# Two transformer blocks on one core: the order of long and short products within a weight slot of an FFN

## What is computed

```
u, g = split(h @ w_up)            # 1024 x 2816 each
g = causal_dwconv(g)              # 3 taps
y = (silu(g) * u) @ w_down        # 2816 x 1024
```

```
y = (silu(x @ wg) * (x @ wu)) @ wd
```

## Time and profile before

| | us |
|---|---|
| median of 3 runs | 1596.24 |
| lowest, highest | 1596.08, 1598.06 |
| the profiled execution, its own time | 1598.12 |
| its span, first to last instruction | 1596.4 |
| busy: TensorE | 1578.2 (99%) |
| busy: VectorE | 1090.8 (68%) |
| busy: ScalarE | 920.0 (58%) |
| busy: GpSimd | 56.7 (4%) |

### The profile page before, as it was taken

The page is one execution under the profiler, slowest core; times in us unless marked ns, Lnnn a source line. Parts: engine busy times, 40 slices in busy tenths (PEclk is TensorE's granted clock), DMA queues, the critical chain, the costliest instruction groups (busy, mean ns, idle before and its releaser), DMA issues.

```text
span 1596.4 us, 23557 instructions
## 1 busy us (share of the span) xinstructions
PE 1578.2 (99%) x9239; PEld 1355.2 (85%) x9239; DVE 1090.8 (68%) x1759; ACT 920.0 (58%) x1553; POOL 56.7 (4%) x98
## 2 busy tenths in 40 slices
PE   7999999999999999999999999999999999999998
PEld 6888888889888888888887788888888889888887
DVE  5877776778676767665677466567666667775665
ACT  5756755567665546644476564457454484674544
POOL 4010000000030000000002100000000000000000
PEclk9999999999999999999999999999999999999999
DMA  8555666555356555666655465665666664456662
GB/s 286 161 158 171 221 226 193 186 163 166 114 182 200 192 186 182 200 187 189 192 164 168 122 204 180 199 191 164 215 190 187 186 198 147 120 177 202 188 188 77
DMA packets 212401, 288.20 MB, mean 181 GB/s; under 512 B 11096, under 2 KB 180382, under 8 KB 212292
## 3 DMA queue, kind: packets, MB, share of 16 engines
q1 hardware_dynamic: 208500, 280.00, 55.6%
q0 software_dynamic: 3792, 6.70, 1.6%
HBM read 284.99 MB, written 3.88 MB: 181 GB/s over the span
## 4 chain that ended last, share of the span: by engine, by line
PE 94%; DVE 2%; DMA 1%; ACT 1%; issue 0%; SPq 0%; POOL 0%; DVEq 0%
PE two L2211 88%; PE two L2288 1%; PE two L2457 1%; DVE w_lo L1483 1%; PE two L2470 1%; DMA x_tok<-in_x 1%; PE two L2480 1%; DVE qk L1839 1%; PE two L2840 0%; PE two L2274 0%; DMA vals<-u_dram 0%; ACT w_hi L864 0%; PE two L2483 0%; DMA u_dram<-aux 0%; DVE misc L1817 0%
## 5 line engine op out<-in xcount | busy, mean ns | idle before, releaser
L2211 PE MATMUL two<-act_parts,w_hi 128*128 128x512 f32 (+1 forms) x2784 | 803.4, 353 | 0.0
L1483 DVE TENSOR_TENSOR w_lo<-raw,w_hi 128x1024 fp32r<-128x1024 f32 (+1 forms) x520 | 612.9, 1220 | 114.7 <-ACT w_hi L864 114.2
L2211 PE MATMUL two<-act_parts,w_lo 128*128 128x256 f32 x2256 | 637.2, 282 | 0.0
L2211 PEld LDWEIGHTS two<-act_parts,w_hi 128*128 128x128 f32 x2784 | 487.6, 189 | 80.8 <-issue 5.4
L864 ACT CAST w_hi<-raw 128x1024 fp32r<-128x1024 f32 (+1 forms) x520 | 516.3, 1048 | 7.0 <-DMA raw<-in_ffn_w_up 4.7
L2211 PEld LDWEIGHTS two<-act_parts,w_lo 128*128 128x128 f32 x2256 | 425.4, 189 | 2.1
L2211 PE MATMUL two<-w_hi,act_parts 128*128 128x512 f32 (+2 forms) x832 | 247.1, 377 | 3.1 <-ACT w_hi L864 3.0
L993 ACT COPY p_sb<-two 128x512 f32<-128x512 f32 x108 | 62.7, 580 | 243.0 <-PE two L2211 243.0
L2211 PE MATMUL two<-w_hi,hid_even 128*128 128x512 f32 x576 | 185.7, 390 | 0.0
L2211 PEld LDWEIGHTS two<-w_hi,act_parts 128*128 128x128 f32 x832 | 151.0, 189 | 32.6 <-ACT w_hi L864 3.4
L1611 DVE TENSOR_TENSOR pt_sb<-two,p_sb 128x512 f32<-128x512 f32 x54 | 37.3, 691 | 194.5 <-ACT p_sb L993 194.5
(11 more groups left out here) (317 smaller groups left out, 1191.9 us busy)
## 6 DMA issues: line engine op xcount, KB each, us to landing
raw<-in_ffn_w_up SPq DMA_DIRECT2D x160, 512.0 KB, 4.1
raw<-in_ffn_w_down SPq DMA_DIRECT2D x132, 512.0 KB, 3.5
raw<-in_ffn_w_gate SPq DMA_DIRECT2D x80, 512.0 KB, 3.8
raw<-in_a_w_in SPq DMA_DIRECT2D x24, 512.0 KB, 4.9
raw<-in_fox_w_in SPq DMA_DIRECT2D x20, 512.0 KB, 3.8
raw<-in_ffn_w_up SPq DMA_DIRECT2D x32, 256.0 KB, 3.7
raw<-in_w_kv SPq DMA_DIRECT2D x12, 512.0 KB, 4.2
raw<-in_mem_w_kv SPq DMA_DIRECT2D x8, 512.0 KB, 11.3
```

Of the source, the lines that this page charges most:

```text
L1483: nc.vector.tensor_tensor(slot(w_lo, t, n), slot(raw, t, n), slot(w_hi, t, n), ALU.subtract).then_inc(lo_done, 1)
L2211: return nc.tensor.matmul(dst, a, w, start=start, stop=stop, skip_group_check=True)
```

## The change

It reorders the products of a slot in `gate_or_up` for s of 2 and more: first the eight long products of the slot, in the order (k, m), and then its eight short products in the same order. For s = 1 the order stays as it was. The number, the operands and the outputs of the products stay the same, each has its LDWEIGHTS as before, and the increment stays on the slot's last product, a short one in both kernels.

```diff
@@ -2336,18 +2336,20 @@
                         t = gate_slots(f, s) + 2 * part + i
                         slot_ready(t)
                         hi, lo = whole_slot(t, 4)
-                        for k in range(4):
-                            for m in range(2):
-                                c, w = 4 * i + k, slice(m * P, (m + 1) * P)
-                                if s == 1:
-                                    d = gate_up(part)[:, m * SEQ:(m + 1) * SEQ]
-                                    mm(d, hi[:, k, w], act_parts[:, 0, c, :], c == 0 and m == 0, False)
-                                    mm(d, hi[:, k, w], act_parts[:, 1, c, :], False, False)
-                                else:
-                                    d = gate_up_wide(part)[:, m * HALF:m * HALF + SEQ]
-                                    mm(gate_up_wide(part)[:, m * HALF:(m + 1) * HALF].rearrange("p (a t) -> p a t", a=2), hi[:, k, w],
-                                       act_parts[:, :, c, :], c == 0, False)
+                        tiles = [(k, 4 * i + k, m, slice(m * P, (m + 1) * P)) for k in range(4) for m in range(2)]
+                        if s == 1:
+                            for k, c, m, w in tiles:
+                                d = gate_up(part)[:, m * SEQ:(m + 1) * SEQ]
+                                mm(d, hi[:, k, w], act_parts[:, 0, c, :], c == 0 and m == 0, False)
+                                mm(d, hi[:, k, w], act_parts[:, 1, c, :], False, False)
                                 ins = mm(d, lo[:, k, w], act_parts[:, 0, c, :], False, c == NCH - 1)
+                        else:
+                            for k, c, m, w in tiles:
+                                mm(gate_up_wide(part)[:, m * HALF:(m + 1) * HALF].rearrange("p (a t) -> p a t", a=2), hi[:, k, w],
+                                   act_parts[:, :, c, :], c == 0, False)
+                            for k, c, m, w in tiles:
+                                ins = mm(gate_up_wide(part)[:, m * HALF:m * HALF + SEQ], lo[:, k, w], act_parts[:, 0, c, :], False,
+                                         c == NCH - 1)
                         ins.then_inc(gu_full if i else w_tm, 1)
 
                 def down(s, b, halves=(0, 1)):
```

## The result

The changed kernel takes 1599.29 us (median of 20 runs), the kernel before 1597.06 beside it: a ratio of 1.0015, 95% interval 1.0008 to 1.0021. It is slower by about 2.2 us, where 1591.3, a gain of 4.9 us, was forecast.

A forecast was written before the change was run, and what follows sets the result against it. TensorE was taken as the bound, busy 1578.2 of 1596.4 us. Rows of like products gave -9.9 and entries +5.0, together -4.9 us, median 1591.3; own range 1587.5 to 1593.5, with rivals 1585 to 1601.5.

The forecast's parts named there:

- Step (1): In a slot's row of eight long products: 0.2267 us each, 1.814 a row, from down steps; bounds 0.22 and 0.24.
- The price of 0.006: In gate and up's alternating order: each long-short pair pays some 0.006 us for the change of length, over 1728 pairs.
- the pair of 0.34: In the alternating order: one pair took 0.34 us, matching 0.2267 and 0.1187, so two segments carry no fixed price.
- Step (2): In a slot's row of eight short products: 0.1187 us each, 0.950 a row, with weight loads hidden.
- Step (3): At 168 entries from shorts into rows of longs: 0.03 us each, +5.0 us; the way back costs nothing.
- Step (4): At slot releases and their readers on SyncE, ScalarE and VectorE: starts 0.02 us earlier a slot, cost nothing.
- Rival B: In a slot's longs: they keep 0.2325 us in a row, entries add 0.03 each; slower, 1601.2 us, chance 0.22.
- Rival A: In gate and up slots: order doesn't matter, a slot stays at 2.81 us, median 1596.2; chance 0.2.
- The rule that the prediction took from the Trainium skill: For TensorE's product distances: columns over 2.4 GHz and 2.5 ns, so a pair is 0.325 in any order, change worth nothing.

The follow-up runs named there:

- alike_new: Changed kernel with the gate and up weight slots placed like all others, a move of 32 columns: 1593.46 us, ratio 0.9977 against the kernel before.
- act_moved: Changed kernel with weight slots unmoved and the activations moved by 32 columns: 1595.51 us beside 1596.81 for the kernel before, a single run.
- adjacent_new: Changed kernel with a chunk's hi and lo activations side by side in SBUF: 1599.2 us, ratio 1.0013 against the kernel before.
- adjacent_old: Kernel before, longs and shorts in turn, with a chunk's hi and lo activations side by side in SBUF: 1596.85 us, ratio 1.0000.
- sweep_new: Changed kernel with a different pair of places for the high and low weights of gate and up in each FFN: 1594.75 us, a single run.
- mixed_new: Changed kernel with only `w_hi` of steps 2 to 10 placed like all other slots: 1595.4 us, ratio 0.9991 against the kernel before.
- quarter_new: Changed kernel with gate and up slots at a third place, 16 columns from either other: 1587.11 us, ratio 0.9941 against the kernel before.
- snake: mixed_new with shorts first in the second slot of each part: 1590.33 us, ratio 0.9959 against the kernel before.
- quarter_snake: quarter_new with shorts first in the second slot of each part: 1583.89 us, ratio 0.9919 against the kernel before.

## Why the prediction was wrong

**Step (1), eight long products in a row, failed.** It took 0.2267 from the down steps, "the row with most of the same kind", and they ran at 0.2329: a row takes 1.863 us for 1.814, 216 x 0.049 = +10.6 us, which is more than the whole gain of 9.9. The reason is shown by alike_new and act_moved: the products of the down steps have their operands at another distance than gate and up have. The code said so. `STANDING_SLOTS` places these slots unlike all others, and the prediction used this for the shorts (0.1187 from the same kind of slot against 0.120 from the other) and not for the longs. A row warned of it as well: the one long product behind a 512-column product takes 0.24. The prediction used it as a bound only, and the bound held the value.

**The price of 0.006 that grouping was to save** fell with it. It was 0.351 in turn less 0.3454, and 0.3454 had the 0.2267 of the other placement in it. In the changed kernel's own rows a pair costs 0.2329 + 0.1192 = 0.3521, which is 0.001 more than the 0.3511 in turn (the mean over all slots before). At the kernels' place the products gain nothing in rows of their own kind, and the small loss is the +2 us.

**The argument from the pair of 0.34** The earlier trace rows didn't carry. Its conclusion, no fixed price of the two segments, is what adjacent_new and adjacent_old show. But a single distance between starts rounded to 0.01 can't exclude a price of 0.006, and it didn't show that a long product can keep 0.2267 there: single distances vary within a row, and only a mean over the pattern is a price.

**Step (2), the shorts**, held nearly: 0.954 us a row for 0.950, which is +0.8 us in all.

**Step (3), entries, was wrong the other way.** At the kernels' own place there are none to be seen: eight longs behind a down take 1.867 us on average and behind shorts 1.862, so the +5.0 is missing. Together: -4.9 + 10.6 - 5.0 + 0.8 = +1.5, against +1.96 in the stretches; the rest is the rounding of 2.81 and 5.46. So the error of 10.6 was partly hidden by one of 5.0. The price of 0.03 was right where longs settle: 1.81 against 1.84 and 1.85 in alike_new. The sum's picture of a slot (2.764, and 0.03 for three slots of four) is 2.787, which alike_new measured; it is the slot of another placement.

**Step (4)**, readers and releases at no cost, held: TensorE has no gap in the stretches of either kernel, its two longest waits are the same to 0.1 us, and so are VectorE's and ScalarE's busy times in the stretches.

**Rival B** had the sign and, by luck, one number: 0.2325 for a long product, measured 0.2329. It had put the whole surplus of a pair on the long product, while in the trace of before the means in turn are 0.2309 for a long and 0.1202 for a short product. Its threshold of 0.2296 was passed. The two segments, which it named, cost nothing, and its entries on top didn't come: +5.0 us for the measured +2.2. Its 1601.2 was 1.9 us too high and not 2.8, since the forecast started from the median of 3 runs, 1596.24, and that of 20 is 1597.06. **Rival A** had a slot's time of 2.81 nearly right, for a reason that fell: the order does matter, by -11 to +2 us, depending on the place. The rule that the prediction took from the Trainium skill, TensorE: Matmul & The Clock Gate, section Back-to-back issue gap, says less on this case than was made of it: the section gives its formula for an isolated product and says of a stream that weight load and product set the spacing together.

On the weight loads the Trainium skill, TensorE: Matmul & The Clock Gate, section Step-by-step: what each phase is for, says that loading the next tile's weights doesn't take SBUF read bandwidth from the running matmul. No run here separates a load from its product, so the rule is not tested. What the runs show is that the two operands' places aren't independent: 32 columns more or less between the standing and the moving operand are 0.2267 or 0.233 us for a 512-column product. That the loads' reading meets the streaming is one way to explain this, and is not shown.

**What stays open:** what in the chip makes the distance count, and why the pairs of places in sweep_new and mixed_new don't add up. The distances within a row come in fixed patterns: in quarter_new the four rows of shorts of a step take 0.91, 0.91, 0.94 and 0.94 us, in each of the steps 2 to 9, though their slots lie alike. mixed_new shows that a product's neighbours count. Step 10 of quarter_new shows that what ran ahead counts: its gate stands behind short products in place of a down, and in all six FFNs its first row of shorts takes 0.944 us for 0.907, eight long products after the difference. How the one leads to the other, no run tells.

## What to carry to other kernels

Before a price is taken from another group of the same shape, ask whether its operands' addresses have the same distance; check the placement code before the row is used. An order that was tuned at one placement has to be tried again at others: here one and the same reordering was +2.0 us at one place and -9 to -11 us at two others, and the best kernel took both. And the dearest step of a sum deserves two rows of unlike origin, or its bound as the value.

## What the hardware showed that was not expected

- The time from one 512-column product to the next depends on how far the two operands' addresses are apart in SBUF: 0.2264 or 0.233 us. The same shift by 32 columns made products whose activations stream faster and products whose activations stand slower. For 256-column products in a row it is 0.120, 0.1187 and, at the place between, 0.1133 or near 0.118. The 0.1133 is the up of step 1 in quarter_new's first FFN, from the first row to the last 30 products in 3.40 us; in the third FFN its 47 distances take 5.53 us, 0.1177 each:

```profile
175.59 0.39 PE L2211 MATMUL two<-act_parts,w_hi 128*128 128x256 f32 x2
...
178.99 0.39 PE L2211 MATMUL two<-act_parts,w_hi 128*128 128x256 f32 x2
```

- The order of 512- and 256-column products is worth up to 0.05 us a slot of sixteen, at the same work and clock and without a wait in the stretches, and its sign depends on the place.
- A row of eight 512-column products takes 0.03 us more behind 256-column ones than behind 512-column ones in alike_new, and nothing more in the changed kernel. Leaving out two of four such passages a step saved 4.9 us over 54 steps at one place (snake) and 3.0 us at another (quarter_snake).
